# Expert weights of a mixture layer: two loads into the output buffers, and a first step in another order

## The chip, the cores and the metric

One core of a Trainium2 chip runs the whole program. The time is the device time of one execution in microseconds; the median of 3 runs of the kernel before is 484.61 us (483.82 to 484.63).

## The reference

One decoder layer over 256 tokens of width 1024, in float32. First come four token mixers (two kinds of attention with 4 heads of 64, a convolution, and a latent attention), fed by one input projection, merged by sigmoid gates and an output projection, and added to the input. Then follows what this case is about, a mixture of experts:

```python
hn = rmsnorm(h, norm2_g)
# router: top group of 4, top 2 experts of its 8, weights for the two
# for every token and each of its two experts e:
y = (silu(hn @ w1[e]) * (hn @ w3[e])) @ w2[e]     # w1, w3: 1024 x 256, w2: 256 x 1024
h = h + sum of weight * y
out = rmsnorm(h, final_g)
```

There are 32 experts. Each has a gate matrix (w1), an up matrix (w3) and a down matrix (w2) of 1 MiB each, so 96 MiB in all, and every expert's weights are read.

## The kernel before

The mixer part takes the first half of the time. TensorE (PE) works on split operands there: ACT writes the high part of a weight into `w_parts` (`WH`), DVE the rest (`WL`), and PE multiplies three combinations. `w_parts` is no longer needed for that when the output projection ends (`tile_done`). From then on it serves in two ways: its first 2048 words of either half are the buffers of the experts' outputs (`y_part`, high and low part), and the two tails behind them are two of the slots for expert weights. The router's small words (`LG`, `RB`, `KEY` and so on) and `PAIRWISE` lie in it too, in words 1024 to 2047 of either half.

**The experts** are worked on in 6 steps of two pairs each (pair 0 and pair 1; `GROUPS` = 12 groups g, g = 2n + pair). In steps 0, 1, 3 and 4 a pair has two experts with up to 64 tokens each, in steps 2 and 5 four experts with up to 32. Steps 0 and 1 take the experts 0 to 7; from step 2 on the order is sorted by the number of tokens, known when `order_ready` is raised.

**The loads.** `LOADS` lists the 96 loads in the order of use: for each group the gate and up matrix of each expert, and then the down matrices. So loads 0 to 3 are the gate and up matrices of group 0, 4 and 5 its down matrices, 6 to 9 and 10, 11 those of group 1, and so on; group 4 has loads 24 to 35, group 5 has 36 to 47. There are 18 slots (`RING`), and load i goes into slot i % 18. SP issues them in one queue, in this order: 0 to 5, and then 6, 7 and 17, during the mixer; 8 to 10 when `w_parts` is free of weights (`w_lo`), 11 to 15 when the output projection has ended (`tile_done`), and 16 (`LATE`) when the router's logits are there (`logits_ps`), since the router's weights lie in its slot. From load 18 on, `freed(i)` waits for the work that read load i - 18: `hid_ps` g + 1 for gate and up matrices (raised when PE ends the gate and up products of group g), `y_ps` 2g + 2 for down matrices (raised when PE ends both halves of the down products of group g). SP takes them strictly in order: a load that waits holds up all behind it. From load 24 (`FIRST_SORTED`) on the expert's number is read from `LIST`.

**PE's order in a step n** (`step`, L1920): the products of pair 0 with gate and up matrices (`hidden(n, 0)`, L1833); the scatter of the step before; the transposes of pair 0's hidden values (L1480); the transposes of the selection (`select_t`); the down products of pair 0 in two halves (L1872); the products of pair 1 (`hidden(n, 1)`); the first two parts of the gather of the next step's tokens (L1796); transposes of pair 1; the third part of the gather, a down product, the fourth, and the second down product.

**DVE's order in a step** (`step`, L1394): the hidden values of pair 0 (L1369, L1372, after ACT's tanh, L807); the sums of the step before; the copy of the transposed values (L1377); weights of the slots; the low parts of pair 0's outputs (L1361, after ACT's high part, L813); then `select_next`, which writes the next step's selection (L1321), weighs it (L1328) and, in step 0, works out the destinations (`choice_sum`, L1254); the hidden values of pair 1; then copies of gathered tokens (L1355), with the copy of pair 1's transposed values between.

PE's `keep_awake` products have no use but to keep it busy.

Of the kernel before, what the change touches and what calls it, by code (L numbers as in the profile page):

```python
# [18 lines left out]
F32 = mybir.dt.float32  # L19
# [7 lines left out]
D = 1024  # L27
T = 256
TT = T // P
# [3 lines left out]
NE = 32  # L33
# [97 lines left out]
def trunk_kernel(nc, A, out):  # L131
    ctx = ExitStack()
    with ctx:
# [7 lines left out]
        def alias(name, of, at, n, dt):  # L141
# [12 lines left out]
            score_ps conv_a_sb logit_ready row_max neg_max prob_exp prob_ready pt_ps pt_sb pv_ps attn_ready  # L154
            gate_t merged tmp_mul merge_hi merge_split
            tile_done h_ready wr_ready h_sq h_root h_rstd hs_hi hs_split hst_ps hst_sb_act hst_sb_dve logits_ps router_exp
            rank_ps total_ps counts_sb sel_ready gather_ps xe_ready key_ready columns_ps places_ready rows_ps order_ready over_ready
            wselt_ps selt_sb hid_ps hid_t hid_ready hidt_ps hidt_sb y_ps y_hi y_split o_ps o_free
            first_gate_half first_down_half final_sq final_root out_ready stored router_chain sel_part sel_chain step_chain x_chain order_chain wsel_part
            slot_weight wsel_ready over_moved warm""".split()  # L160
# [132 lines left out]

        ro = carver(last(0), SLOT)
        WR = ro(KD * 36).rearrange("p (k n) -> p k n", k=KD)
        rt = carver(alias("router_words", "w_parts", D, D, F32), D)
        RB_O32 = 20 + 9 * 2 + 2 * 8 + 8 * 16 + 64
        LG = rt(72).rearrange("p (t n) -> p t n", t=TT)
        RB = rt(320)
        KEY, BASE, CAPS = (rt(NE) for _ in range(3))  # L300
        COLS = rt(2)
        PAIRWISE = alias("router_pairs", "w_parts", NPART * PARTW + D, D, F32).rearrange("p (a b) -> p a b", a=NE)
        PLACES, COLUMNS, KEY_ROW = PAIRWISE, COLS, KEY[0:1, :]

        vv = carver(VEC[:, :], 258)
# [131 lines left out]
        LAST = len(LOADS)  # L437
        HALVED = (LAST - 6, LAST - 5, LAST - 2, LAST - 1)

        def ring_loads(r):  # L440

            return len(range(r, len(LOADS), RING))

        def wide(pair, k):

# [25 lines left out]
        def _(sp):  # L471
# [15 lines left out]

            def load_expert(i, expert):

                sp.dma_start(ring_slot(i % RING), (e_gate, e_up, e_down)[LOADS[i][1]][expert]).then_inc(exp_in[i % RING], 16)  # L490

            def rows(name):
                return ROWP[ROWS[name]:ROWS[name] + {"conv_w": 62, "b_gate": 32, "gkv": 1}.get(name, 2), :]
# [1 line left out]
            for n in range(UNITS):  # L495
                load_unit(n)
                if 0 <= n - 1 - NIN < NGATE:
                    load_branch(n - 1 - NIN)
                if n == NRAW - 1:

                    sp.dma_start(rows("conv_w"), A["conv_w"][0].rearrange("k (j p) -> (k j) p", p=P)).then_inc(s.params_in, 16)
                    for name, key in (("conv_b", "conv_b"), ("ln_g", "conv_ln_g"), ("ln_b", "conv_ln_b"), ("gq", "mla_gq"),
                                      ("gkv", "mla_gkv")):
                        sp.dma_start(rows(name), A[key][0].rearrange("(j p) -> j p", p=P)).then_inc(s.params_in, 16)
                    sp.dma_start(rows("b_gate"), A["b_gate"][0].rearrange("i (m p) -> (i m) p", p=P)).then_inc(s.params_in, 16)
                    sp.dma_start(TABS[:, P:NKEEP], A["tables"][:, P:NKEEP]).then_inc(s.tables_in, 16)
                    sp.dma_start(MTABS, A["tables"][:, NKEEP:NTAB]).then_inc(s.tables_in, 16)
                    sp.dma_start(G2, A["norm2_g"][0].rearrange("(p k) -> p k", k=KD)).then_inc(s.norm2_in, 16)

                    for j in range(2):  # L510
                        wuq = A["mla_wuq"][0, j * P:(j + 1) * P, :].rearrange("p (h c) -> p h c", h=HEADS)
                        sp.dma_start(WUQ[:, j, 0:256].rearrange("p (h c) -> p h c", h=HEADS), wuq[:, :, 0:64]).then_inc(s.wmla_in, 16)
                        for a in range(2):
                            sp.dma_start(WUQ[:, j, 256 + 64 * a:320 + 64 * a].rearrange("p (b c) -> p b c", b=2),
                                         wuq[:, a::2, 64:96]).then_inc(s.wmla_in, 16)
                    wukv = A["mla_wukv"][0].rearrange("p (h a c) -> p h a c", h=HEADS, a=2)
                    for a in range(2):
                        sp.dma_start(WUKV[:, a * 256:(a + 1) * 256].rearrange("p (h c) -> p h c", h=HEADS), wukv[:, :, a, :])\
                            .then_inc(s.wmla_in, 16)
                    sp.dma_start(BF, A["b_forget"][0].partition_broadcast(P)).then_inc(s.bias_in, 16)  # L520
                    sp.dma_start(BR[:, 0:4], A["b_router_group"][0].partition_broadcast(P)).then_inc(s.bias_in, 16)
                    sp.dma_start(BR[:, 4:36], A["b_router_expert"][0].partition_broadcast(P)).then_inc(s.bias_in, 16)
                if PREFETCH_AT <= n < PREFETCH_AT + 6:
                    load_expert(n - PREFETCH_AT, LOADS[n - PREFETCH_AT][0])
                if n == APART_AT:
                    sp.wait_ge(s.attn_ready, len(PAIRS))
                    sp.wait_ge(s.conv_out, 2)
                if APART_AT <= n < APART_AT + 3:
                    i = (6, 7, LATE + 1)[n - APART_AT]
                    load_expert(i, LOADS[i][0])  # L530

            sp.wait_ge(s.branch_ps, NGATE)
            sp.wait_ge(s.merged, NGATE - 4)
# [1 line left out]
            sp.dma_start(WR[:, :, NG:36], A["w_router_expert"][0].rearrange("(p k) n -> p k n", k=KD)).then_inc(s.router_in, 16)  # L535

            sp.wait_ge(s.w_lo, 2 * UNITS)
            for i in (8, 9, 10):
                load_expert(i, LOADS[i][0])
            sp.wait_ge(s.tile_done, TT)  # L540
            for i in (11, 12, 13, 14, 15):
                load_expert(i, LOADS[i][0])
            sp.wait_ge(s.logits_ps, 1)
            load_expert(LATE, LOADS[LATE][0])

            def freed(i):

                _, kind, g = LOADS[i - RING]
                if kind < 2:
                    sp.wait_ge(s.hid_ps, g + 1)  # L550
                else:
                    sp.wait_ge(s.y_ps, 2 * g + 2)

            for i in range(RING, FIRST_SORTED):
                freed(i)
                load_expert(i, LOADS[i][0])
            sp.wait_ge(s.order_ready, 1)
            expert = {}
            for i in range(FIRST_SORTED, len(LOADS)):
                position, kind, _ = LOADS[i]  # L560
                if position not in expert:
                    expert[position] = sp.value_load(LIST[0:1, position:position + 1], min_val=0, max_val=NE - 1)
                freed(i)
                if i not in HALVED:
                    load_expert(i, expert[position])
                elif i + 1 in HALVED:
                    for h in range(2):
                        words = slice(h * SLOT // 2, (h + 1) * SLOT // 2)
                        for which in (i, i + 1):
                            position, kind, _ = LOADS[which]  # L570
                            freed(which)
                            sp.dma_start(ring_slot(which % RING)[:, words], (e_gate, e_up, e_down)[kind][expert[position]][:, words])\  # L572
                                .then_inc(exp_in[which % RING] if h else s.first_down_half if kind == 2 else s.first_gate_half, 16)

            sp.wait_ge(s.over_ready, 1)
            count = sp.value_load(LIST[0:1, NE:NE + 1], min_val=0, max_val=MAX_OVER)
# [263 lines left out]
        def _(dve):  # L840
# [369 lines left out]
                dve.wait_ge(s.order_chain, oc[0])  # L1210

            DT = EALL.rearrange("p t g e -> p t (g e)")
            DT2 = RB[:, RB_O32:RB_O32 + TT * NE].rearrange("p (t e) -> p t e", t=TT)
            index = tab("iota")[:, 0:NE]

            def across(v):
# [60 lines left out]
                olink(V.tensor_tensor(DT2, DT2, tokens(BASE), ALU.add))  # L1277

            def destinations():
                choice_sum(DEST, DT2, PAIRWISE[:, 0:2, :])  # L1280

            def overflow_list(n):

# [191 lines left out]
        def _(pe):  # L1475
# [335 lines left out]
            def arrived(position, kind, half=1):  # L1811

                i = LOAD_OF[position, kind]
                if half == 0 and i in HALVED:
                    pe.wait_ge(s.first_down_half if kind == 2 else s.first_gate_half, 32)
                else:
                    pe.wait_ge(exp_in[i % RING], 16 * (i // RING + 1))

            def hidden(n, pair):

# [3 lines left out]
                for k in range(KD):  # L1824
# [5 lines left out]
                        pe.wait_ge(s.xe_ready, n * 8 + k + 2)  # L1830
                    for position, at, width in tiles(n, pair):
                        x = xe[:, k, pair * P + at:pair * P + at + width]
                        ins = mm(bank[pair][at:at + width, :], x, wide(LOAD_OF[position, 0] % RING // 2, k),  # L1833
                                 start=(k == 0), stop=(k == KD - 1), skip_group_check=True)
                ins.then_inc(s.hid_ps, 1)

# [22 lines left out]
            def down(n, pair, half):  # L1859
# [8 lines left out]
                after(pe, s.y_split, n * 4 + (half + 1 if pair else half - 1))  # L1868
                for j in range(2):
                    for position, at, width in tiles(n, pair):  # L1870
                        w = ring_slot(LOAD_OF[position, 2] % RING)[:, j * D + half * 512:j * D + half * 512 + 512]
                        ins = mm(bank[2 + half][at:at + width, :], HTT[:, pair, j, at:at + width], w,  # L1872
                                 start=(j == 0), stop=(j == 1), skip_group_check=True)
                ins.then_inc(s.y_ps, 1)
# [1 line left out]
            def down_last(n, pair):  # L1876

                pe.wait_ge(s.hidt_sb, n * 2 + pair + 1)
                for j in range(2):
                    for position, _, _ in tiles(n, pair):  # L1880
                        arrived(position, 2, j)
                    for half in range(2):
                        if j == 0:
                            pe.wait_ge(s.y_split, n * 4 + half + 1)
                        for position, at, width in tiles(n, pair):
                            w = ring_slot(LOAD_OF[position, 2] % RING)[:, j * D + half * 512:j * D + half * 512 + 512]
                            ins = mm(bank[2 + half][at:at + width, :], HTT[:, pair, j, at:at + width], w,
                                     start=(j == 0), stop=(j == 1), skip_group_check=True)
                        if j:
# [30 lines left out]
            def step(n):  # L1920
# [2 lines left out]
                hidden(n, 0)  # L1923
                if n:
                    scatter(n - 1)
                hidden_t(n, 0)
                select_t(n, 0)
                down(n, 0, 0)
# [2 lines left out]
                if not more:  # L1931
                    pe.wait_ge(s.o_free, n * 4 + 2)
                    pe.wait_ge(s.hidt_sb, n * 2 + 1)
                    for i in range(4):
                        scatter_part(n, i, 0, SCATTER_LAST[i], True, False)
                hidden(n, 1)
                if more:
                    gather_part(n + 1, 0, outputs=n * 4 + 2)
                    gather_part(n + 1, 1, outputs=n * 4 + 2)
# [80 lines left out]
```

## Time and profile before

| | |
|---|---|
| median of 3 runs | 484.61 us |
| the profiled execution | 485.79 us, its span 483.8 us |
| PE busy | 443.7 us (92%) |
| DVE busy | 282.0 us (58%) |
| ACT busy | 157.1 us (32%) |
| read from HBM | 139.58 MB, 291 GB/s over the span |
| mean granted TensorE clock | 0.982 |

The span goes from the first instruction to the last; 1.99 us of the execution lie outside it. PE's matmuls are pipelined and their ends modelled, so 92% does not say that PE bounds the time. The chain that ended last is put down to PE for 76% of the span and to DMA for 15%. In the rows below a clock (PEclk) of 1.00 is full speed.

### The profile page before, as it was taken

How to read it: one execution, taken by the hardware profiler on the slowest of the kernel's cores; microseconds unless marked ns; L12 is line 12 of the kernel's file. 1: busy time of each engine (PE TensorE's matmuls, PEld its weight loads, DVE VectorE, ACT ScalarE, POOL GpSimd, SP SyncE). 2: the span in 40 equal slices, each digit the busy share in tenths (PEclk: the TensorE clock that was granted, in tenths of full speed). 3: DMA queues.
4: the chain of work that ended last, by engine and by line, in shares of the span. 5: the costliest groups of instructions: out<-in, count | busy, mean ns of one | idle time of the engine just before them, and what ended most of it. 6: DMA issues, size and time to landing. Idle time of an engine off the chain costs nothing.

```text
span 483.8 us, 7556 instructions
## 1 busy us (share of the span) xinstructions
PE 443.7 (92%) x2941; PEld 317.6 (66%) x2941; DVE 282.0 (58%) x591; ACT 157.1 (32%) x282; POOL 3.1 (1%) x12
## 2 busy tenths in 40 slices
PE   3999999999999999999989899999959999969882
PEld 2999899889999899998876254354424354424321
DVE  3749668878788558475477353644564644614115
ACT  5644556543644437344462100110010110010004
POOL 1100000000000000000000000000000000000000
PEclk9999999999999999999999899999988999989998
DMA  8784556886844548933396799999999999999982
GB/s 292 195 270 156 175 157 216 288 306 209 281 133 154 174 146 278 321 127 99 106 425 253 286 379 416 417 409 373 423 422 423 421 421 419 423 421 420 416 331 89
DMA packets 54486, 141.13 MB, mean 292 GB/s; under 512 B 8523, under 2 KB 39474, under 8 KB 42674
## 3 DMA queue, kind: packets, MB, share of 16 engines
q1 hardware_dynamic: 54162, 140.57, 77.1%
q8 instruction: 24, 0.39, 0.3%
q10 hardware_dynamic: 288, 0.07, 0.1%
q14 instruction: 12, 0.10, 0.1%
HBM read 139.58 MB, written 1.05 MB: 291 GB/s over the span
## 4 chain that ended last, share of the span: by engine, by line
PE 76%; DMA 15%; DVE 3%; SPq 3%; issue 1%; ACT 1%; DVEq 0%
PE bank L1833 14%; PE bank L1494 10%; PE bank L1495 9%; PE bank L1496 9%; PE bank L1872 6%; PE bank L1716 6%; DMA scratch<-in_w_exp_up 5%; DMA part_words<-in_w_exp_up 4%; DMA expert_slots<-in_w_exp_down 4%; PE bank L1480 2%; PE bank L1730 2%; SPq L572 2%; DMA expert_slots<-in_w_in 2%; PE bank L1732 2%; PE bank L1731 2%; PE bank L1909 2%
## 5 line engine op out<-in xcount | busy, mean ns | idle before, releaser
L1494 PE MATMUL bank<-act_hi,w_parts 128*128 128x256 f32 x384 | 112.1, 292 | 1.0 <-DVE act_lo L867 1.0
L1496 PE MATMUL bank<-act_lo,w_parts 128*128 128x256 f32 x384 | 108.6, 283 | 0.0
L1495 PE MATMUL bank<-act_hi,w_parts 128*128 128x256 f32 x384 | 108.5, 283 | 0.0
L1833 PE MATMUL bank<-expert_slots,merged_t 128*64 128x512 f32 (+1 forms) x352 | 89.2, 618 | 10.5 <-DMA part_words<-in_w_exp_up 4.9
L860 DVE TENSOR_TENSOR w_parts<-expert_slots,w_parts 128x1024 fp32r<-128x1024 f32 (+4 forms) x63 | 72.0, 1171 | 21.6 <-ACT w_parts L637 21.6
L1494 PEld LDWEIGHTS bank<-act_hi,w_parts 128*128 128x128 f32 x384 | 73.6, 192 | 3.3 <-issue 1.6
L1495 PEld LDWEIGHTS bank<-act_hi,w_parts 128*128 128x128 f32 x384 | 73.2, 191 | 0.3
L1496 PEld LDWEIGHTS bank<-act_lo,w_parts 128*128 128x128 f32 x384 | 73.1, 190 | 0.0
L637 ACT ACTIVATE w_parts<-expert_slots 128x1024 fp32r<-128x1024 f32 (+4 forms) x63 | 62.1, 1020 | 29.0 <-issue 14.2
L1833 PEld LDWEIGHTS bank<-expert_slots,merged_t 128*64 128x64 f32 (+1 forms) x352 | 27.6, 127 | 54.9 <-issue 54.5
L813 ACT ACTIVATE w_parts<-bank,vectors 128x512 fp32r<-128x512 f32 x24 | 16.5, 688 | 91.2 <-PE bank L1872 84.9
L1833 PE MATMUL bank<-scratch,merged_t 128*32 128x512 f32 (+1 forms) x96 | 44.0, 613 | 0.0
L1369 DVE SCALAR_TENSOR_TENSOR scratch<-scratch,bank 128x256 f32<-128x256 f32 x12 | 5.1, 422 | 66.7 <-ACT scratch L807 66.7
L807 ACT ACTIVATE scratch<-bank 128x256 f32<-128x256 f32 x12 | 4.6, 386 | 98.3 <-PE bank L1833 98.3
L1361 DVE SCALAR_TENSOR_TENSOR w_parts<-bank,vectors,w_parts 128x512 fp32r<-128x512 f32 x24 | 18.0, 748 | 27.3 <-ACT w_parts L813 27.2
L1833 PE MATMUL bank<-part_words,merged_t 128*64 128x512 f32 (+1 forms) x64 | 31.1, 643 | 0.0
L712 ACT ACTIVATE scratch<-bank,vectors 128x256 f32<-128x256 f32 x32 | 13.4, 470 | 54.0 <-PE bank L1496 54.0
L1872 PE MATMUL bank<-expert_slots,scratch 128*64 128x512 f32 (+1 forms) x144 | 28.4, 622 | 2.2 <-DVE scratch L1377 1.6
L1716 PE MATMUL bank<-scratch,expert_slots 128*128 128x256 f32 x128 | 30.2, 379 | 0.0
L1716 PEld LDWEIGHTS bank<-scratch,expert_slots 128*128 128x128 f32 x128 | 23.2, 190 | 2.5
L886 DVE SCALAR_TENSOR_TENSOR scratch<-scratch,vectors 128x256 f32<-128x256 f32 x60 | 24.7, 480 | 0.0
L944 DVE SCALAR_TENSOR_TENSOR scratch<-scratch,bank 128x512 f32<-128x512 f32 x12 | 8.2, 687 | 27.9 <-ACT scratch L712 27.4
(285 smaller groups left out, 646.7 us busy)
## 6 DMA issues: line engine op xcount, KB each, us to landing
expert_slots<-in_w_exp_gate SPq DMA_DIRECT2D x21, 1024.0 KB, 10.1
expert_slots<-in_w_exp_up SPq DMA_DIRECT2D x21, 1024.0 KB, 12.1
expert_slots<-in_w_exp_down SPq DMA_DIRECT2D x20, 1024.0 KB, 19.3
expert_slots<-in_w_gate SPq DMA_DIRECT2D x16, 1024.0 KB, 6.2
expert_slots<-in_w_in SPq DMA_DIRECT2D x8, 1024.0 KB, 6.6
scratch<-in_w_exp_down SPq DMA_DIRECT2D x8, 1024.0 KB, 18.7
scratch<-in_w_exp_gate SPq DMA_DIRECT2D x6, 1024.0 KB, 16.5
scratch<-in_w_exp_up SPq DMA_DIRECT2D x6, 1024.0 KB, 17.8
```

The costliest lines, as they stand in the source:

```text
L637: ins = nc.scalar.activation(part_slice(WH, q, where), raw, ACT.Copy)
L712: nc.scalar.activation(TMPB[:, m * T:(m + 1) * T], (PA, PB)[g % 2][:, m * T:(m + 1) * T], ACT.Tanh, bias=HGB[:, c:c + 1], scale=0.5).then_ ...
L813: nc.scalar.activation(y_part(WH, pair, half), bank[2 + half][:, :], ACT.Copy, scale=WS[:, pair:pair + 1]).then_inc(s.y_hi, 1)
L860: ins = V.tensor_tensor(part_slice(WL, q, where), raw, f32(part_slice(WH, q, where)), ALU.subtract)
L886: ins = V.scalar_tensor_tensor(CACC[:, j, :], src, w, CACC[:, j, :], ALU.mult, ALU.add)
L1361: V.scalar_tensor_tensor(y_part(WL, pair, half), bank[2 + half][:, :], WS[:, pair:pair + 1], f32(y_part(WH, pair, half)), ALU.mult, ALU.su ...
L1494: mm(dst, wh, xh, start=first, stop=False)
L1495: mm(dst, wl, xh, start=False, stop=False)
L1496: return mm(dst, wh, xl, start=False, stop=last)
L1716: ins = mm(BRB[:, m * T:(m + 1) * T], wb[:, j, m * 128:(m + 1) * 128], YT[b][:, j, :], start=(j == 0), stop=(j == 1))
L1833: ins = mm(bank[pair][at:at + width, :], x, wide(LOAD_OF[position, 0] % RING // 2, k), start=(k == 0), stop=(k == KD - 1), skip_group_chec ...
L1872: ins = mm(bank[2 + half][at:at + width, :], HTT[:, pair, j, at:at + width], w, start=(j == 0), stop=(j == 1), skip_group_check=True)
```

## The change

Two things are changed in the experts' part.

The first: loads 4 and 5 (the down matrices of group 0) leave the ring. They go into `once`, which is the output buffers of both halves of `w_parts` (words 0 to 2047), and have a semaphore of their own (`once_in`). The ring's 18 slots are dealt to the other 94 loads in order (`RING_ORDER`, `TURN`): load i has turn i for i under 4 and i - 2 behind. Place 16 is then load 18 and place 17 load 19. SP issues loads 4 and 5 last before the waits, behind load 18. Loads 20 to 23 are freed by loads 0 to 3; load i from 24 on is freed by load i - 18, as before. The router's words that lay in the output buffers move: to the buffer of transposed hidden values (`HTTV`), to `WSEL2` and to `FAR_RANK`.

The second: in step 0 PE works on `hidden(0, 1)` right behind `hidden(0, 0)`, ahead of the transposes and down products of pair 0. The other steps and the orders of DVE and ACT stay.

```diff
         ro = carver(last(0), SLOT)
         WR = ro(KD * 36).rearrange("p (k n) -> p k n", k=KD)
-        rt = carver(alias("router_words", "w_parts", D, D, F32), D)
+        rt = carver(HTTV, 512)
...
-        COLS = rt(2)
-        PAIRWISE = alias("router_pairs", "w_parts", NPART * PARTW + D, D, F32).rearrange("p (a b) -> p a b", a=NE)
+        ww = carver(WSEL2, 256)
+        PAIRWISE = ww(3 * NE).rearrange("p (a b) -> p a b", a=3)
+        COLS = ww(2)
+        CHOICE = ww(TT * NE).rearrange("p (t e) -> p t e", t=TT)
...
+        ONCE = (4, 5)
+        once = alias("output_words", "w_parts", 0, 2 * NPART * PARTW, F32).rearrange("p (a n) -> p a n", a=2)[:, :, 0:SLOT]
+        RING_ORDER = [i for i in range(len(LOADS)) if i not in ONCE]
+        TURN = {i: turn for turn, i in enumerate(RING_ORDER)}
+
         def ring_loads(r):
-            return len(range(r, len(LOADS), RING))
+            return len(range(r, len(RING_ORDER), RING))
+
+        def load_slot(i):
+            return once[:, ONCE.index(i), :] if i in ONCE else ring_slot(TURN[i] % RING)
...
             def load_expert(i, expert):
-                sp.dma_start(ring_slot(i % RING), (e_gate, e_up, e_down)[LOADS[i][1]][expert]).then_inc(exp_in[i % RING], 16)
+                sp.dma_start(load_slot(i), (e_gate, e_up, e_down)[LOADS[i][1]][expert])\
+                    .then_inc(s.once_in if i in ONCE else exp_in[TURN[i] % RING], 16)
+
+            def load_place(r):
+                load_expert(RING_ORDER[r], LOADS[RING_ORDER[r]][0])
...
             sp.wait_ge(s.w_lo, 2 * UNITS)
-            for i in (8, 9, 10):
+            for r in (8, 9, 10):
+                load_place(r)
+            sp.wait_ge(s.tile_done, TT)
+            for r in (11, 12, 13, 14, 15):
+                load_place(r)
+            sp.wait_ge(s.logits_ps, 1)
+            load_place(LATE)
+            for i in ONCE:
                 load_expert(i, LOADS[i][0])
-            sp.wait_ge(s.tile_done, TT)
-            for i in (11, 12, 13, 14, 15):
-                load_expert(i, LOADS[i][0])
-            sp.wait_ge(s.logits_ps, 1)
-            load_expert(LATE, LOADS[LATE][0])

             def freed(i):
-                _, kind, g = LOADS[i - RING]
+                _, kind, g = LOADS[RING_ORDER[TURN[i] - RING]]
...
-            for i in range(RING, FIRST_SORTED):
+            for i in range(RING + len(ONCE), FIRST_SORTED):
                 freed(i)
                 load_expert(i, LOADS[i][0])
...
-            DT2 = RB[:, RB_O32:RB_O32 + TT * NE].rearrange("p (t e) -> p t e", t=TT)
+            DT2 = FAR_RANK
...
-                choice_sum(DEST, DT2, PAIRWISE[:, 0:2, :])
+                choice_sum(DEST, DT2, CHOICE)
...
                 if half == 0 and i in HALVED:
                     pe.wait_ge(s.first_down_half if kind == 2 else s.first_gate_half, 32)
+                elif i in ONCE:
+                    pe.wait_ge(s.once_in, 16 * len(ONCE))
                 else:
-                    pe.wait_ge(exp_in[i % RING], 16 * (i // RING + 1))
+                    pe.wait_ge(exp_in[TURN[i] % RING], 16 * (TURN[i] // RING + 1))
...
                 hidden(n, 0)
                 if n:
                     scatter(n - 1)
+                else:
+                    hidden(n, 1)
                 hidden_t(n, 0)
                 select_t(n, 0)
                 down(n, 0, 0)
...
-                hidden(n, 1)
+                if n:
+                    hidden(n, 1)
```

The other places that named `i % RING` or `ring_slot` of a load use `TURN[i]` and `load_slot` in the same way.

## Rows read from the trace of the kernel before

**Rows 1.** The page, the span in 40 equal slices: GB/s moved.

```profile
...
GB/s 292 195 270 156 175 157 216 288 306 209 281 133 154 174 146 278 321 127 99 106 425 253 286 379 416 417 409 373 423 422 423 421 421 419 423 421 420 416 331 89
```

**Rows 2.** Windows: length, busy PE, PEld, DVE, ACT, POOL; PEclk, DMA share, GB/s.

```profile
...
252.00:255.00 3.00, 1.63 (x13) 1.21 (x11) 1.74 (x12) 0.20 (x1) 0.00 (x0) 1.00 0.99 418
263.00:268.00 5.00, 5.00 (x26) 1.58 (x22) 2.43 (x13) 0.00 (x0) 0.00 (x0) 1.00 0.00 0
270.00:273.00 3.00, 2.70 (x12) 0.89 (x12) 1.18 (x3) 0.00 (x0) 0.00 (x0) 0.75 0.89 371
273.00:276.00 3.00, 3.00 (x12) 0.87 (x10) 1.38 (x3) 0.69 (x1) 0.00 (x0) 0.68 1.01 426
...
330.00:335.00 5.00, 4.56 (x20) 3.31 (x20) 3.67 (x7) 0.39 (x1) 0.00 (x0) 1.00 0.97 349
345.00:350.00 5.00, 5.00 (x45) 3.22 (x38) 1.76 (x5) 0.39 (x1) 0.00 (x0) 1.00 1.01 423
```

**Rows 3.** The chain that ended last: start us, us, engine, what, line.

```profile
...
261.41 7.04 PE bank L1833 x32
...
269.34 0.43 DVE scratch L1372
269.82 0.52 PE bank L1480 x2
...
270.84 3.09 PE bank L1872 x8
...
276.60 6.87 PE bank L1833 x32
...
289.77 1.87 PE bank L1872 x8
...
303.36 0.35 DVE scratch L1377
...
306.06 1.87 PE bank L1872 x8
...
340.02 20.88 DMA part_words<-in_w_exp_up
...
452.57 17.82 DMA expert_slots<-in_w_exp_down
```

**Rows 4.** SP's issues in order of time: start us, us of one issue.

```profile
...
268.46 0.33 SPq L490 DMA_DIRECT2D expert_slots<-in_w_exp_gate  x1
...
283.68 0.36 SPq L490 DMA_DIRECT2D scratch<-in_w_exp_gate  x1
...
323.59 0.38 SPq L490 DMA_DIRECT2D expert_slots<-in_w_exp_up  x1
...
330.17 0.34 SPq L490 DMA_DIRECT2D scratch<-in_w_exp_gate  x1
```

**Rows 5.** Issues of 268:269, 283:284, 323:324, 330:331: last number, us to landing.

```profile
...
expert_slots<-in_w_exp_gate SPq DMA_DIRECT2D x1, 1024.0 KB, 4.8
...
scratch<-in_w_exp_gate SPq DMA_DIRECT2D x1, 1024.0 KB, 6.0
...
expert_slots<-in_w_exp_up SPq DMA_DIRECT2D x1, 1024.0 KB, 10.1
...
scratch<-in_w_exp_gate SPq DMA_DIRECT2D x1, 1024.0 KB, 7.6
```

**Rows 6.** PE and DVE in order of time; in brackets the idle time before.

```profile
...
254.03 0.41 PE L1769 MATMUL bank<-router_words,shape_tables 128*128 128x32 f32 x2 [1.37 <-DVE router_words L1151]
...
278.04 0.75 DVE L1321 TENSOR_TENSOR select<-scratch,shape_tables 128x256 fp32r<-128x256 f32 x2
...
284.02 0.42 DVE L1369 SCALAR_TENSOR_TENSOR scratch<-scratch,bank 128x256 f32<-128x256 f32 x1 [3.01 <-ACT scratch L807]
284.47 0.42 DVE L1372 SCALAR_TENSOR_TENSOR scratch<-scratch,bank 128x256 f32<-128x256 f32 x1
...
285.40 0.41 PE L1480 MATMUL bank<-shape_tables,scratch 128*128 128x128 f32 x2
```

More of the change, by code:

```diff
@@ L156, in trunk_kernel @@
             tile_done h_ready wr_ready h_sq h_root h_rstd hs_hi hs_split hst_ps hst_sb_act hst_sb_dve logits_ps router_exp
-            rank_ps total_ps counts_sb sel_ready gather_ps xe_ready key_ready columns_ps places_ready rows_ps order_ready over_ready
+            rank_ps total_ps counts_sb sel_ready gather_ps xe_ready once_in key_ready columns_ps places_ready rows_ps order_ready over_ready
             wselt_ps selt_sb hid_ps hid_t hid_ready hidt_ps hidt_sb y_ps y_hi y_split o_ps o_free
@@ L523, in _ @@
                 if PREFETCH_AT <= n < PREFETCH_AT + 6:
-                    load_expert(n - PREFETCH_AT, LOADS[n - PREFETCH_AT][0])
+                    load_place(n - PREFETCH_AT)
                 if n == APART_AT:
@@ L528, in _ @@
                 if APART_AT <= n < APART_AT + 3:
-                    i = (6, 7, LATE + 1)[n - APART_AT]
-                    load_expert(i, LOADS[i][0])
+                    load_place((6, 7, LATE + 1)[n - APART_AT])
             sp.wait_ge(s.branch_ps, NGATE)
@@ L537, in _ @@
             sp.wait_ge(s.w_lo, 2 * UNITS)
-            for i in (8, 9, 10):
-                load_expert(i, LOADS[i][0])
-            sp.wait_ge(s.tile_done, TT)
-            for i in (11, 12, 13, 14, 15):
-                load_expert(i, LOADS[i][0])
-            sp.wait_ge(s.logits_ps, 1)
-            load_expert(LATE, LOADS[LATE][0])
+            for r in (8, 9, 10):
[6 more added lines that the diff above has]
+            for i in ONCE:
+                load_expert(i, LOADS[i][0])
             def freed(i):
-                _, kind, g = LOADS[i - RING]
+                _, kind, g = LOADS[RING_ORDER[TURN[i] - RING]]
                 if kind < 2:
@@ L571, in _ @@
                             freed(which)
-                            sp.dma_start(ring_slot(which % RING)[:, words], (e_gate, e_up, e_down)[kind][expert[position]][:, words])\
-                                .then_inc(exp_in[which % RING] if h else s.first_down_half if kind == 2 else s.first_gate_half, 16)
+                            sp.dma_start(load_slot(which)[:, words], (e_gate, e_up, e_down)[kind][expert[position]][:, words])\
+                                .then_inc(exp_in[TURN[which] % RING] if h else s.first_down_half if kind == 2 else s.first_gate_half, 16)
             sp.wait_ge(s.over_ready, 1)
@@ L1832, in hidden @@
                         x = xe[:, k, pair * P + at:pair * P + at + width]
-                        ins = mm(bank[pair][at:at + width, :], x, wide(LOAD_OF[position, 0] % RING // 2, k),
+                        ins = mm(bank[pair][at:at + width, :], x, wide(TURN[LOAD_OF[position, 0]] % RING // 2, k),
                                  start=(k == 0), stop=(k == KD - 1), skip_group_check=True)
@@ L1870, in down @@
                     for position, at, width in tiles(n, pair):
-                        w = ring_slot(LOAD_OF[position, 2] % RING)[:, j * D + half * 512:j * D + half * 512 + 512]
+                        w = load_slot(LOAD_OF[position, 2])[:, j * D + half * 512:j * D + half * 512 + 512]
                         ins = mm(bank[2 + half][at:at + width, :], HTT[:, pair, j, at:at + width], w,
@@ L1885, in down_last @@
                         for position, at, width in tiles(n, pair):
-                            w = ring_slot(LOAD_OF[position, 2] % RING)[:, j * D + half * 512:j * D + half * 512 + 512]
+                            w = load_slot(LOAD_OF[position, 2])[:, j * D + half * 512:j * D + half * 512 + 512]
                             ins = mm(bank[2 + half][at:at + width, :], HTT[:, pair, j, at:at + width], w,
```

## The prediction

> **What bounds the kernel now.** I read the 40 slices first, then stretches of the expert part, then the chain that ended last, then SP's issues with their times to landing, and last the first expert step on PE and DVE.
>
> The slices [rows 1] show low transfer rates in the mixer and rates near 420 GB/s from slice 24 on. All 32 experts are loaded, 96 loads of 1 MiB, so from there the time looks like bytes over rate. At the 423 GB/s of 345 to 350 us [rows 2] one load takes 1.0486 MB / 423 GB/s = 2.48 us. The same rows hold the hole that the change aims at: nothing is moved in 263 to 268 us. The 18 slots are full or on their way, and SP stands at the wait for the end of the first gate and up products.
>
> The chain [rows 3] shows who is late where. The first products run from 261.41 for 7.04 us, to 268.45. PE then waits for ACT and DVE until its transposes at 269.82 (1.37 us), down products follow at 270.84, and the second pair's products at 276.60. From there to 339.58 the chain lies almost wholly on PE. At 340.02 it passes to a load that takes 20.88 us to land, and from there the queue is long; the last load, issued at 452.57, lands 17.82 us later, at 470.39. So there are two stages: up to about 331 us PE releases slots and the queue runs nearly dry; behind it transfers bound everything. The rates say it too: 349 GB/s in 330 to 335, 423 in 345 to 350 [rows 2].
>
> The hinge is load 42 (counted from 0 in the order of use). It is issued at 330.17, when the gate and up products of the third step's first pair end, and lands 7.6 us later, at 337.8; load 41 landed at 323.59 + 10.1 = 333.7 [rows 4, 5]. Behind load 42 come 53 loads: 337.8 + 53 x 2.48 = 469.2, against 470.39 seen, so there is hardly a hole behind it. The end follows load 42 one to one.
>
> **The change, part by part.**
>
> *Two more places.* Loads 4 and 5 (the first two down weights) go into the output buffers, issued behind load 18. They take 2 x 2.48 = 5.0 us of the hole: the queue works 5 us longer before it runs dry. They are read at about 276, so nobody waits for them. Each issue costs SP about 0.4 us [rows 4], while it had nothing to do.
>
> *What the places free.* Loads 20 to 23 now lie where loads 0 to 3 did and are all issued at 268.46, at the event that before released 18 to 21. For load 24 and on the turn number drops by 2, and so does the occupant: each waits for exactly the load it waited for before (load i for load i - 18). So the 2 MiB are ahead, but no later slot is released sooner by the places alone. Before, load 24 was issued at 283.68, when the queue had just run dry. If PE's events stay, the later events, from 291.6 (worked out below) to 330.17, find a shorter queue, and the 5.0 us turn into new holes between 290 and 331.
>
> *Both products in a row.* The second pair's 6.87 us [rows 3] now start at 268.45 and end at 275.32. That issues loads 24 to 27 about 8 us sooner than at 283.68. With 20 to 23 (10 us, from 268.46 + 4.8 - 2.48 = 270.8 [rows 5]) they keep the queue busy to about 290.6. Load 28 waits for the end of the step's down products, at 289.77 + 1.87 = 291.64 before. So that time counts, and I work it out on PE.
> - Transposes of pair 0 start at 275.32; 0.52 us [rows 3] bring the copy to 275.84. The wait of 1.37 us is covered by the second products.
> - In step 1, at full clock, the time from the copy to the end of the second down product is 306.06 + 1.87 - 303.36 = 4.57 us [rows 3]. Here that gives 280.41. Before it was 276.60. So this point is 3.81 us later.
> - What hid behind the second products is open now. DVE's low halves and the next selection come after these down products: before, the selection was ready at 278.04 + 0.75 = 278.79 [rows 6], 2.19 us after 276.60. PE will wait from 280.41 to 282.60 before it can gather.
> - On DVE the destinations follow; behind them, before, DVE waited 3.01 us for pair 1's products, from 281.01 to 284.02 [rows 6]. The shift of 3.81 eats these 3.01 and leaves 0.80 us. Its result, ready at 284.89 before, comes at 285.69. PE took it up at 285.40 only, because it was gathering, which hides 0.51 more; with 0.05 for the semaphore (269.77 to 269.82 [rows 3]) the transposes start at 285.75, 0.35 us late. PE, done gathering (1.93 us, from 276.60 + 6.87 = 283.47 to 285.40 before) at 284.53, waits 1.2 us.
> - Behind them every step is as before, so the down products end at 292.0.
>
> That the two waits of 1.7 us and the slow clock (PEclk 0.75 and 0.68 in 270 to 276, thus 3 x 0.25 + 3 x 0.32 = 1.7 us lost [rows 2]) go, and waits of 3.4 us come, is the same sum: about 0.35 us to the bad. The release of load 42 moves with it. Whether the clock falls in the new waits the trace doesn't say: a wait of 1.37 us that ended at 254.03 [rows 6] was not followed by a fall, the one of 1.37 us at 268.45 was, and a new one is 2.2 us long. From both sides: 0 to 1.7 us. The 1.7 us were lost in 3.4 us at half speed; for 1.2 of such 3.4 PE would stand anyway, a third, so I take 1.1 us if it falls.
>
> *Relief at the hinge.* Load 42 landed 7.6 us after its issue. With an idle queue load 18 took 4.8 us, and load 24 with one just dry 6.0 [rows 5]. Behind load 41 it could land at 333.7 + 2.48 = 336.2 at the soonest, from its issue at 335.0; the other 1.6 us are a slow start. If the queue in front is shorter, up to 1.2 us of backlog go, and with the slow start 2.8. Against that, new dry starts come at loads 28 and 30, each costing something like load 24's. So from both sides: 0 to 2.8 us gained. I take 0.65, half the backlog, since load 42's own slow start is the nearest row and most of what is ahead is lost in the holes before it.
>
> *A rule of the skill.* Rows first: idle to landing 4.8 us, 2.3 more than the 2.48 of a load in a full queue [rows 5]. The Trainium skill (SBUF — State Buffer, "The DMA setup-cost knee") says that each transfer pays a fixed cost of about 2 us, whatever its size. By it alone load 42 lands 4.5 us behind its issue, which would make the end about 3 us sooner; the trace's 7.6 and 6.0 us disagree for a queue that has just run dry.
>
> *The router's words* move to other buffers, with the same instructions in the same order: 0. Nothing of them is written over before its last use, so I see no wait for it.
>
> **Sum.** +0.35 (release) - 0.65 (relief) = -0.3 us. The profiled execution took 485.79, its span 483.8 and 1.99 around it; it would take 485.5. The median, 484.61, is 1.18 below it, so 484.3.
>
> **The rivals.**
> - *Relief in full.* Load 42 lands 4.8 us behind its issue: 330.17 + 0.35 + 4.8 = 335.3 instead of 337.8, 2.5 sooner: 482.1. For it: the queue in front is surely shorter after 290. Against: loads 24 and 42 both had slow starts. The skill's rule above is this rival. Chance 0.20.
> - *The bytes count in full.* If transfers bound from 268 on, 5.0 us go: 479.6. Against: the hole-free queue needs releases that PE doesn't give sooner. Chance 0.08.
> - *Slower: the clock falls in the exposed wait.* PE stands 2.2 us at 280.4 and 1.2 at 284.5. If the granted clock goes to half there, transposes, gathers and a down product run slow and load 28 to 42 are released 0.35 + 1.1 us later: 486.1 with no relief. It decides if the fall reaches past 285.7, since gathering before it has slack. Chance 0.20, and 0.02 more for loads 4 and 5 landing late (over 9 us of margin), about as slow.
> - *Forecast:* 0.50.
>
> **How the numbers follow.** What a measurement of this kernel can tell from no change is 0.2%, 0.97 us. Faster: 0.20 + 0.08 = 0.28. Slower: 0.22. Within: 0.50. The range leaves out the full 5.0 us and the worst of the clock: 482.1 to 486.1. The forecast's own range is 483.7 to 485.5.
>
> **What would show it.** Right: transfers 5 us into the hole; loads 20 to 27 issued by about 277; PE waiting some 2 us ahead of the gather and 1 us ahead of pair 1's transposes; holes in the queue at 290 to 294 and near 299; the third step's first release at 330.5. Wrong: the second products not starting at once; no wait ahead of the gather; the queue full between 290 and 331 or the step's last down product ending before 290 (then 479.6 is near); load 42 landing 5 us behind its issue; or a half clock around 283 to 288.

## The result and the profile after

The change makes the kernel a little slower: median 485.73 us (20 runs) against 484.53 for the kernel before (20 runs). The ratio, estimated from all runs and not from the two medians alone, is 1.0028, 95% interval [1.0015, 1.0041], so +1.4 us (0.7 to 2.0). The forecast was 484.3, no difference that can be measured, and gave "slower" a chance of 0.22. The profiled execution of the changed kernel has a span of 483.2 us; both its first expert products and its end lie earlier than those of before on the clock of the trace, so I measure everything from the start of the first gate and up products: 261.41 before [rows 3], 259.76 after. From there to the span's end it is 222.4 us before and 223.4 after.

The page after, the slices (granted clock and DMA share in tenths, GB/s):

```profile
...
PEclk9999999999999999999989989999988999989998
DMA  8793566787736358832498886999999999999982
GB/s 294 205 321 98 170 194 218 270 298 233 269 111 204 123 192 285 308 109 78 166 422 370 332 364 267 395 380 370 425 420 422 420 421 420 422 420 422 415 339 89
...
```

The chain that ended last, after (start us, us, engine, line); its lines 1851, 1496, 1890 and 1812 are the 1833, 1480, 1872 and 1796 of before:

```profile
...
259.76 13.88 PE bank L1851 x64
273.64 0.45 PE bank L1496 x2
274.11 0.43 DVE scratch L1393
274.59 1.94 PE bank L1890 x8
...
276.90 1.89 PE bank L1890 x8
278.81 0.69 ACT w_parts L829
279.57 0.63 issue
280.20 0.76 DVE select L1337 x2
281.00 0.58 PE bank L1812
...
288.82 1.87 PE bank L1890 x8
290.69 6.87 PE bank L1851 x32
...
339.06 21.01 DMA expert_slots<-in_w_exp_up
...
451.87 17.83 DMA expert_slots<-in_w_exp_down
```

The two products now run in one piece of 13.88 us. Where the chain of before stayed on PE, it leaves it behind the down products: ACT and DVE have to finish the outputs and write the selection before the gather can begin. PE and DVE in order of time show the length of that wait, in brackets:

```profile
...
280.20 0.75 DVE L1337 TENSOR_TENSOR select<-scratch,shape_tables 128x256 fp32r<-128x256 f32 x2
...
281.00 0.58 PE L1812 MATMUL bank<-select,act_hi 128*128 128x256 f32 x1 [2.24 <-DVE select L1337]
```

2.24 us, where 2.2 was forecast. The windows after (length; busy PE, PEld, DVE, ACT, POOL; PEclk, DMA share, GB/s):

```profile
...
260.00:265.00 5.00, 5.00 (x26) 1.69 (x24) 3.67 (x18) 0.96 (x3) 0.00 (x0) 1.00 0.87 359
265.00:267.00 2.00, 2.00 (x12) 0.61 (x10) 0.00 (x0) 0.18 (x1) 0.00 (x0) 1.00 0.01 4
278.00:281.00 3.00, 0.76 (x4) 0.00 (x0) 1.91 (x5) 0.96 (x2) 0.00 (x0) 0.98 0.98 415
281.00:284.00 3.00, 3.00 (x14) 3.00 (x15) 2.76 (x10) 0.00 (x0) 0.00 (x0) 0.50 1.04 434
288.00:291.00 3.00, 3.00 (x19) 1.44 (x20) 1.54 (x3) 0.68 (x2) 0.00 (x0) 1.00 0.10 33
297.00:299.00 2.00, 2.00 (x11) 1.25 (x8) 0.94 (x3) 0.39 (x1) 0.00 (x0) 1.00 0.34 82
329.00:334.00 5.00, 4.60 (x23) 3.35 (x20) 3.62 (x7) 0.39 (x1) 0.00 (x0) 1.00 0.87 293
344.00:349.00 5.00, 5.00 (x47) 3.07 (x40) 1.63 (x4) 0.38 (x1) 0.00 (x0) 1.00 1.02 423
```

The old hole of the queue is filled up to 265 us, and two new ones stand at 288 to 291 and 297 to 299, where forecast. The granted clock is at its lower level, 0.50, in 281 to 284, in and behind the new wait. And load 42 finds the queue no quicker than before: 293 GB/s in 329 to 334, against 349 in 330 to 335 [rows 2]. SP's issues after:

```profile
...
266.81 0.33 SPq L501 DMA_DIRECT2D expert_slots<-in_w_exp_gate  x1
...
273.84 0.36 SPq L501 DMA_DIRECT2D expert_slots<-in_w_exp_gate  x1
...
290.88 0.34 SPq L501 DMA_DIRECT2D expert_slots<-in_w_exp_gate  x1
...
329.22 0.34 SPq L501 DMA_DIRECT2D expert_slots<-in_w_exp_gate  x1
```

Load 42 is issued 329.22 - 259.76 = 69.46 us behind the first products; before it was 330.17 - 261.41 = 68.76. So by these two traces the change costs 0.70 us there, and 1.0 at the end, where the ratio says 1.4. The experiments found that the 0.70 is too small, since the trace of before isn't typical of its kernel.

### The profile page after: what moved, and what is told of

The parts are those of the page before. It is cut to its first block, busy times and chain, and to the rows that moved or that the text cites. A ratio compares the mean times of both kernels' runs of the same rounds, so it can differ in the third digit from the quotient of the medians.

```text
span 483.2 us, 7556 instructions
## 1 busy us (share of the span) xinstructions
PE 443.7 (92%) x2941; PEld 318.6 (66%) x2941; DVE 281.9 (58%) x591; ACT 156.8 (32%) x282; POOL 2.1 (0%) x12
## 4 chain that ended last, share of the span: by engine, by line
PE 76%; DMA 15%; DVE 3%; SPq 3%; ACT 1%; issue 1%; DVEq 0%
PE bank L1851 14%; DMA expert_slots<-in_w_exp_up 10%; PE bank L1510 10%; PE bank L1511 9%; PE bank L1512 9%; PE bank L1732 6%; PE bank L1890 5%; DMA expert_slots<-in_w_exp_down 4%; PE bank L1812 2%; PE bank L1746 2%; SPq L588 2%; PE bank L1748 2%; PE bank L1496 2%; PE bank L1747 2%; PE bank L1927 2%; DMA expert_slots<-in_w_in 2%
## 5 line engine op out<-in xcount | busy, mean ns | idle before, releaser
L1510 PEld LDWEIGHTS bank<-act_hi,w_parts 128*128 128x128 f32 x384 | 72.8, 189 | 4.0 <-DVE w_parts L876 2.1
L1511 PEld LDWEIGHTS bank<-act_hi,w_parts 128*128 128x128 f32 x384 | 72.4, 189 | 0.3
L1851 PE MATMUL bank<-scratch,merged_t 128*32 128x512 f32 (+1 forms) x128 | 58.0, 607 | 5.1 <-DMA expert_slots<-in_w_exp_up 5.1
L1851 PEld LDWEIGHTS bank<-scratch,merged_t 128*32 128x32 f32 (+1 forms) x128 | 15.7, 125 | 24.9 <-issue 24.9
L1890 PE MATMUL bank<-expert_slots,scratch 128*64 128x512 f32 (+1 forms) x112 | 27.0, 602 | 1.3 <-DVE scratch L1393 1.3
L1812 PE MATMUL bank<-select,act_hi 128*128 128x256 f32 x80 | 22.5, 313 | 2.2 <-DVE select L1337 2.2
```

Of the source, the lines that this page charges most:

```text
L1510: mm(dst, wh, xh, start=first, stop=False)
L1511: mm(dst, wl, xh, start=False, stop=False)
L1812: mm(dst, xh4[:, t, k, :], sel, start=(t == 0), stop=False)
L1851: ins = mm(bank[pair][at:at + width, :], x, wide(TURN[LOAD_OF[position, 0]] % RING // 2, k), start=(k == 0), stop=(k == KD - 1), skip_grou ...
```

## Experiments

All ratios are to the kernel before, run on the same chip in the same job. "Issue of 42" is the time from the start of the first products to the issue of load 42, from each kernel's profile; "span's end" is counted from the same start.

| kernel | order of the first step | loads 4, 5 | ratio [95%] | issue of 42 | span's end | clock falls in step 0 |
|---|---|---|---|---|---|---|
| before, profile 1 | old | ring | 1 | 68.76 | 222.39 | yes, at the first wait |
| before, profiles 2 and 3 (e9, e10) | old | ring | | 67.18, 67.16 | 222.34, 221.18 | no |
| e1_places | old | buffers | 0.9998 [0.9984, 1.0012] | 67.20 | 221.46 | no |
| e2_order | new | ring | 1.0022 [1.0006, 1.0039] | 69.26 | 224.17 | no |
| changed, profiles 1 and 2 (e11) | new | buffers | 1.0028 [1.0015, 1.0041] | 69.46, 69.63 | 223.44, 223.01 | yes, at the wait for DVE |
| e3_early | new, selection early | buffers | 0.9941 [0.9922, 0.9961] | 66.30 | 218.59 | no |
| e4_order_early | new, selection early | ring | 0.9953 [0.9936, 0.9970] | 66.33 | 219.81 | no |

The kernel before was profiled three times. The issue of load 42 differs by 1.6 us between profile 1 and the other two, and the ends by 1.2 us, but not in step with it: e9 issues load 42 1.58 us sooner than profile 1 and ends 0.05 us sooner. So an end in one profile is known to about 1 us only, and differences at the end are taken from the ratios.

**The two halves alone.** e1_places is the changed kernel with PE's order of before:

```diff
                 if n:
                     scatter(n - 1)
-                else:
-                    hidden(n, 1)
...
-                if n:
-                    hidden(n, 1)
+                hidden(n, 1)
```

> The changed kernel with PE's old order in the first step: loads 4 and 5 in the output buffers, router words moved, second products behind the down products again. Theory A (PE's releases bind up to load 42; the 2 MiB lead dies in holes of the queue): no release from load 24 on moves, so the end stays, 484.5 (ratio 0.999 to 1.001), with load 24 issued as late as before and a longer hole ahead of it. Rival B (bytes bind from 268 us on): 5 us less, 479.6. Rival C (the loss of the change comes from the places, by a slower start at load 42): about 1 us more, 485.5.

Measured: 484.72 us, ratio 0.9998. The places alone are worth nothing, and cost nothing, to within 0.8 us (interval 0.9984 to 1.0012). Theory A stands against B and C: the 5 us of transfers are done earlier and then waited away, as its windows show (154 GB/s in 278 to 283, while SP stands at load 24):

```profile
...
261.00:264.00 3.00, 3.00 (x15) 1.03 (x16) 2.65 (x13) 1.26 (x4) 0.00 (x0) 1.00 1.03 429
...
278.00:283.00 5.00, 5.00 (x31) 2.48 (x28) 1.83 (x8) 0.38 (x1) 0.00 (x0) 1.00 0.47 154
```

e2_order is the kernel before with the other half, the same lines of `step` put in.

> The kernel before with both gate and up products of the first step in a row, and nothing else. Theory A (the loss is the wait that the order exposes on DVE, 0.35 us, and the clock's fall in it, 0.35 to 1.1 us): 0.7 to 1.4 us more, 485.2 to 485.9, ratio about 1.002; PE waits some 2.2 us ahead of the gather. Rival C (the places cost it): no change, 484.5.

Measured: 485.83, ratio 1.0022, or +1.1 us (0.3 to 1.9): the loss is the order's. A share of the places under the new order, 1.0028 against 1.0022, is not resolved. But in its profile the clock didn't fall, and load 42 was still issued at 69.26, 2.1 us later than in e1_places. Theory A had the place right and its parts wrong: 0.35 us and a fall were to be the price, and it was 2.1 without a fall. Its chain:

```profile
...
259.83 13.88 PE bank L1833 x64
...
276.98 1.89 PE bank L1872 x8
278.89 0.70 ACT w_parts L813
...
280.28 0.76 DVE select L1321 x2
...
283.28 0.43 DVE scratch L1369
283.74 0.43 DVE scratch L1372
284.21 0.50 PE bank L1480 x2
...
288.68 1.87 PE bank L1872 x8
290.55 6.87 PE bank L1833 x32
```

Its issue of load 42 (329.09 - 259.83 = 69.26):

```profile
...
329.09 0.34 SPq L490 DMA_DIRECT2D scratch<-in_w_exp_gate  x1
```

From 278.87 to 284.21 this chain is ACT's and DVE's. Step 0's down products end 290.55 - 259.83 = 30.72 us behind the first products; 30.93 in the changed kernel, 30.23 in the first profile of before, and 28.64 to 28.66 in the profiles of the old order without a fall (e1, e7 to e10).

**The wait for DVE taken away.** In e3_early DVE writes step 1's selection and works out the destinations behind the first hidden values, while PE is in its 13.88 us of products, and weighs the selection at the end of the step:

```diff
...
                 hidden(n, 0)
+                if early is not None:
+                    early()          # the two writes of SEL, destinations()
...
                 y_low(n, 1, 1)
+                if late is not None:
+                    late()           # waits for wselt_ps 2, then weigh_quad(1)
```

e4_order_early is the same on e2_order.

> The changed kernel, with DVE's selection of step 1 and the destinations done right behind the first hidden values, while PE is in the second products and DVE idle, and the weighing of that selection at the end of step 0. Nothing is left out. Theory A (the exposed wait on DVE ate what the order gives): the gather follows the down products at once, step 0 ends some 3 us sooner, load 28 and all releases up to load 42 too, and the end comes 2.5 to 2.9 us sooner than before, 481.7 (ratio 0.994 to 0.995). Rival D (load 42 lands late whatever its release, since the queue starts slowly or is bound by bytes): under 1 us gained, 483.7 to 484.5.

> As e3_early but with the kernel before's slots: loads 4 and 5 in the ring. Theory A: PE is sooner by the same 2.9 us, but SP stands at load 22 until the first down products end (280.4), the queue has a hole of 2 us there, and from then on bytes bind: load 42 lands about 335 to 336 instead of 337.8, so 1.5 to 2.8 us gained, 481.7 to 483. If the places matter once PE is sooner, this is slower than e3_early by up to 1.5 us; rival E (places are worth nothing in either case): the same as e3_early.

Measured: 481.38 (0.9941) and 482.41 (0.9953). Both beat the kernel before, e3_early by 2.9 us (1.9 to 3.8), and by their ratios the changed one too. Its chain has no DVE step of selection left (the two DVE lines behind ACT are the outputs' low half and pair 1's hidden values), and the down products end at 288.47 - 260.71 = 27.76:

```profile
...
260.71 13.88 PE bank L1865 x64
...
277.91 1.89 PE bank L1904 x8
279.83 0.69 ACT w_parts L829
280.55 0.75 DVE w_parts L1377
281.30 0.34 DVE scratch L1385
...
288.47 6.87 PE bank L1865 x32
```

This is the cause shown by taking it away: the order isn't bad in itself, it stripped the cover from 3 us of DVE (30.72 less 27.76). No run has the early selection with the old order. There the selection was ready 4.68 us before the gather wanted it (278.79 [rows 6], 276.60 + 6.87 = 283.47 [rows 3]), so it should gain nothing; that is argued, not shown. Whether the places add anything under the better order, 0.9941 against 0.9953, lies within the intervals.

**The clock.** e1_places had the same order on PE as before, and was 1.56 us quicker to load 42. The difference that its rows showed was the clock in step 0. So I filled the wait, and took more profiles.

> The kernel before once more, for its profile. Theory F (the clock's fall at PE's first wait in step 0, which the first profile of before shows, is not the rule: three other kernels with the same order on PE up to there don't show it): no fall at the wait of 1.37 us, load 42 issued 67.2 us behind the first products. Rival G (it is the rule in this kernel): the fall, and 68.8 us.

> As e9_before_again, a further execution: theory F no fall and 67.2 us, rival G a fall and 68.8 us.

> The changed kernel once more, for its profile. Theory F: load 42 issued 69.2 to 69.5 us behind the first products whether the clock falls in the wait ahead of the gather or not, since in e2_order it didn't and the number was 69.26.

Load 42 came 67.18 and 67.16 us behind the first products, without a fall in step 0: theory F of the expectations, in which the fall is not the rule. The chain of e9_before_again in step 0, beside [rows 3]:

```profile
...
261.46 7.04 PE bank L1833 x32
...
269.87 0.52 PE bank L1480 x2
...
270.89 1.94 PE bank L1872 x8
...
273.20 1.87 PE bank L1872 x8
275.06 6.87 PE bank L1833 x32
```

Its issue of load 42 (328.64 - 261.46 = 67.18):

```profile
...
328.64 0.34 SPq L490 DMA_DIRECT2D scratch<-in_w_exp_gate  x1
```

The down products that took 3.09 us in the first profile take 1.94 at full clock, and the second products start at 13.60 us instead of 15.19. Of six profiles with this order on PE and this wait left open (before three times, e1, e7 and e8), one shows the fall, the one that I predicted from. (e5 and e12, below, don't show it either, but their wait is filled.) The changed kernel's second profile gave 69.63 with a fall.

e5_fill_before and e12_fill3_before put products of no use into the wait:

```diff
                 if n:
                     scatter(n - 1)
+                else:
+                    keep_awake(1, 6, T)      # e12: keep_awake(1, 3, T)
```

> The kernel before with 6 products of no use (256 columns, 0.23 us each) on PE behind the first gate and up products of step 0, where it waits 1.37 us for ACT and DVE. Theory F (the clock's fall at that wait, seen in the profile of before and not in that of e1_places with the same order on PE, comes in only a part of the executions; it cost the profiled one 1.6 us and the median less): the clock stays at 1.00 in step 0 and load 42 is issued 67.2 us behind the first products (68.76 before); the median falls by what part of executions have it, 0 to 1.5 us, 483.1 to 484.6. Rival G (the fall is in every execution of before): 1.5 us less, 483.1, outside noise.

> The kernel before with 3 products of no use (0.46 us each, as e5_fill_before showed, 1.38 us together) in PE's first wait of step 0, so that the wait is filled and hardly exceeded. Theory F: the clock stays at 1.00 there, load 42 is issued 67.2 to 67.4 us behind the first products, and the median is that of before or up to 0.5 us under it, since few executions have the fall. Rival G (nearly all executions of before have it): 0.9 to 1.5 us under before.

I had read the duration of one such product off by half. Six took 2.86 us and made PE 1.1 us late (load 42 at 68.30); 485.45, ratio 1.0015 [0.9998, 1.0031], which says nothing of the fall. Three took 1.49 us: load 42 at 67.19, 483.87, ratio 0.9989 [0.9974, 1.0003]. That nearly all executions of before have the fall (G) is shut out by the profiles; the medians alone don't shut it out, since a gain of up to 1.3 us by never having the fall is not told from none.

e6_fill_after had 8 such products ahead of the changed kernel's gather and 5 ahead of pair 1's transposes.

> The changed kernel with 8 products of no use in the wait ahead of the gather of step 0 and 5 in the wait ahead of pair 1's transposes. Theory (of the change's loss the wait on DVE is the larger part, the clock's fall in it 0.35 us): the clock stays at 1.00 between 275 and 295, load 42 is issued 69.2 us behind the first products instead of 69.46, and the median is 0.2 to 0.5 us under the changed kernel's, about 485.3. Rival (the clock explains the whole loss): 484.5.

The same mistake of size: the 8 took 3.72 us in a wait of 2.24, and the 5 took 2.32 in one of about 1. The clock stayed at 1.00, but load 42 was issued at 71.32: 488.03, ratio 1.0077 [1.0048, 1.0105]. It can't say what the fall costs there. The nearest rows are e2_order's 69.26 without a fall, against 69.46 and 69.63 with one: 0.2 to 0.4 us, from one profile against two, and with the places different as well.

**Who binds, and until when.** Nine products of no use, 4.15 us and not 2.1, on PE behind `hidden(n, 0)` of step 1 or of step 3 of the kernel before:

```diff
                 hidden(n, 0)
+                if n == 1:                   # e8: n == 3
+                    keep_awake(1, 9, T)
```

> The kernel before with 9 products of no use (2.1 us) on PE in step 1, behind the products of pair 0: ahead of load 42's release. Theory A (PE's releases bind up to there, one to one): 2.1 us more, 486.7. Rival B (bytes bind): no change.

> The same 2.1 us of products of no use, but in step 3, where the queue is 20 us long. Theory A (transfers bind behind load 42, PE has slack there): no change, 484.6. Rival: 2.1 us more, if PE still sets the end.

In step 1: load 42 issued at 332.06 - 261.06 = 71.00, 3.8 us later than the 67.2 of its kind, and 487.16, ratio 1.0050 [1.0025, 1.0076], +2.4 us:

```profile
...
332.06 0.34 SPq L490 DMA_DIRECT2D scratch<-in_w_exp_gate  x1
```

In step 3: 485.11, ratio 1.0017 [0.9999, 1.0035], at most 1.7 us of the 4.15, and its profile ends 221.5 us behind the first products, as e1_places and e12_fill3_before do (e9 and e10: 222.3 and 221.2). So there are the two stages of the prediction, but the coupling ahead of load 42 looks weaker than one to one: 2.4 of 3.8, with an interval of 1.2 to 3.7 that comes close to it.

## Why the prediction was wrong

**Right.** The places give nothing by themselves: load 24 and all behind it wait for what they waited for before, and the lead dies in new holes (288 to 291 and 297 to 299 after, 278 to 283 in e1_places). The two stages with load 42 between them. The wait ahead of the gather (2.24 for 2.2 us), and DVE's chain as its cause; the wait ahead of pair 1's transposes is 0.96 us in e2_order, where 1.2 was forecast, and gone in the changed kernel's two profiles, whose slow gather lasts until then. The changed kernel's own times came out well: load 42 was to be issued 330.5 - 261.41 = 69.1 us behind the first products and was at 69.46. Loads 4 and 5 were there long before their use, and the router's words cost nothing (e1_places holds both).

**The step that failed** is the sum at the end of "Both products in a row": that two waits of 1.7 us and a slow clock's 1.7 us go and waits of 3.4 us come, "the same sum: about 0.35 us to the bad". (As written there, 3.4 against 3.4 gives 0; the 0.35 comes from the working above it.) For the one execution that they were taken from the terms are nearly right: step 0 was forecast to end at 292.0 - 261.41 = 30.59 us, and e2_order, without a fall, ends it at 30.72. But the slow clock is no part of most executions of the kernel before: 5 of the 6 profiles with its order and its wait don't have it. Against these the new order loses 30.72 - 28.66 = 2.06 us in step 0 and 69.26 - 67.18 = 2.1 us at load 42 without a fall, and 2.3 to 2.5 with the one that the changed kernel's two profiles have. I took what one profile in six shows for a cost that the change would remove. The trace had a warning: the wait of 1.37 us ended at 254.03 had no fall behind it [rows 6], the one of the same length at 268.45 had, and I weighed that only for the new kernel. With an execution without the fall as the base, the same sum gives +0.35 + 1.56 = 1.9 us.

**The relief at load 42**, -0.65 us, was neither shown nor refuted. From the issue of load 42 to the landing of load 51 it took 30.73 us before and 30.85 after; over the profiles it is 30.2 to 32.1 with the old order (before three times, e1, e8, e12) and 29.8 and 30.9 in the changed kernel. That scatter is larger than the term. So 1.9 less 0.65 is 1.3, near the measured 1.4, but only the first part is measured. The 2.1 us lost at load 42, times the 2.4 of 3.8 that e7_delay1 passed on to the end, give 1.3 us as well, without any relief; the runs don't tell the two readings apart.

**The rival "slower"** had the sign and a wrong mechanism: the clock did fall in the exposed wait, in both profiles of the changed kernel, and cost 0.2 to 0.4 us at load 42, not 1.1. A good part of it lay over gathers behind which PE had to wait for DVE anyway: pair 1's transposes started at 24.86 us (284.62) against 24.38 in e2_order (284.21), counted from the first products. **"Relief in full"**: load 28 after, with the queue idle, landed 4.7 us behind its issue, load 42 7.7 us. The Trainium skill's fixed cost of about 2 us (SBUF — State Buffer, "The DMA setup-cost knee") fits load 28 (2.48 + 2.2). It doesn't by itself give the time of load 42, which took 6.4 to 8.9 us in the fourteen profiles. **"One to one"** is not borne out: 2.4 us of 3.8 in e7_delay1, and e3_early gains more at the end than at load 42.

Open: e3_early gains 2.9 us at the end with only 0.9 us at load 42. Its last load lands at 206.3 us behind the first products, against 207.3 in e12, 207.7 in e10, 208.0 in e8 and 208.8 in e9, and in its profile and e4's the last stores land about 1 us sooner behind their issue than in the others. Of the first the earlier issue of loads 24 to 41 is a likely reason, not tested; for the second I have none.

## What to carry to other kernels

Before a stall or a slow clock in one profile is booked as something that a change removes, take the profile of the unchanged kernel again, or look for it in another stretch: what only some executions have is no gain in the median. When work is moved ahead of a wait to cover it, list what the moved work covered where it stood, and move that cover's dependents too: here three microseconds of another engine's work came to lie open, and doing them in its new idle time turned a loss of 0.28% into a gain of 0.59%. Two more buffers were worth nothing here, since the releases behind them came when they had come before.

## What the runs showed of the hardware

A fall of TensorE's granted clock is a matter of the execution, not of the kernel alone: the kernel before shows it in step 0 in one profile of three. The Trainium skill says that the clock's monitor runs freely, without regard to the kernel's start, and that the count of slow matmuls varies from run to run (TensorE: Matmul & The Clock Gate, Part 1). The traces agree with the second; the monitor itself no run here shows. Falls also came ahead of the experts, between 246 and 258 us, in 9 of the 14 profiles. e9_before_again, the kernel before, has one there, where its first profile has 1.00:

```profile
...
252.00:255.00 3.00, 2.58 (x14) 2.31 (x15) 1.85 (x9) 0.00 (x0) 0.00 (x0) 0.76 1.00 421
255.00:258.00 3.00, 3.00 (x16) 2.73 (x15) 1.92 (x1) 0.00 (x0) 0.00 (x0) 0.67 1.03 429
```

There the first expert products start 17.4 us behind the router's, against 15.8 in the first profile of before: 1.6 us in this one execution, and a part of the spread of 483 to 488 us. In the other thirteen profiles, eight of which have such a fall, it is 15.8 to 16.2 us, so most of these falls cost at most 0.4.

A product of 128x128 by 256 columns in float32 took 0.46 to 0.50 us of PE at full clock (nine in 4.15 us, three in 1.49), as two instructions; the count in a timeline row is of instructions. I had taken an instruction for a product.
